# Row factors of the MLP sent by way of HBM, and a new order of work on the last rows

## The reference, cut to what matters

```
def rmsnorm(x, g):
    y = x * rsqrt(mean(x * x, axis=-1) + 1e-6)
    return y * g

x = x + mixed @ w_out                    # mixed: attention and SSM branches, gated
h = rmsnorm(x, g_mlp)                    # x is (512, 1024)
x = x + square(relu(h @ w1)) @ w2        # w1 (1024, 4096), w2 (4096, 1024)
out = rmsnorm(x, g_final)
```

## Time and profile before

| | |
|---|---|
| median of 3 runs | 762.37 us (762.04 to 762.8) |
| the profiled execution | 762.46 us, span 760.6 us |
| granted TensorE clock | 0.999 of full speed |
| PE busy | 744.7 us, 98% of the span |
| DVE busy | 498.1 us, 65% |
| ACT busy | 359.5 us, 47% |
| POOL busy | 54.0 us, 7% |
| HBM | 125 GB/s over the span |

### The profile page before, as it was taken

The page is one execution under the profiler, slowest core; times in us unless marked ns, Lnnn a source line. Parts: engine busy times, 40 slices in busy tenths (PEclk is TensorE's granted clock), DMA queues, the critical chain, the costliest instruction groups (busy, mean ns, idle before and its releaser), DMA issues.

```text
span 760.6 us, 10038 instructions
## 1 busy us (share of the span) xinstructions
PE 744.7 (98%) x3754; PEld 609.2 (80%) x3754; DVE 498.1 (65%) x937; ACT 359.5 (47%) x630; POOL 54.0 (7%) x51
## 2 busy tenths in 40 slices
PE   5999999999999999999999999999999999999996
PEld 4878888777777777888888888888888888888884
DVE  4679999665556673436752667656676567646687
ACT  7524631265556663732421755434443345334454
POOL 3210000000000100000000110011000200020014
PEclk9999999999999999999999999999999999999999
DMA  7673339932223430236238563688177935796322
GB/s 249 197 163 119 100 109 165 202 104 72 70 69 119 159 111 2 84 110 249 84 111 236 124 167 83 166 244 198 56 166 234 229 91 110 196 247 145 83 50 111
DMA packets 99505, 106.19 MB, mean 140 GB/s; under 512 B 10540, under 2 KB 68576, under 8 KB 98432
## 3 DMA queue, kind: packets, MB, share of 16 engines
q1 hardware_dynamic: 93120, 87.05, 40.0%
q0 software_dynamic: 5504, 16.78, 12.1%
q10 hardware_dynamic: 832, 1.71, 1.1%
HBM read 89.70 MB, written 5.34 MB: 125 GB/s over the span
## 4 chain that ended last, share of the span: by engine, by line
PE 93%; DVE 3%; ACT 1%; issue 1%; DMA 1%; POOL 0%; SPq 0%; DVEq 0%; ACTq 0%
PE ps L1642 28%; PE ps L1644 28%; PE ps L1643 27%; PE ps L1932 3%; PE ps L1913 2%; PE ps L1922 1%; DMA mixA<-in_x 1%; PE ps L1717 1%; DVE w_lo L1435 1%; PE ps L1846 1%; ACT w_hi L636 1%; PE ps L1829 1%; DVE x L1484 1%; PE ps L1806 0%; PE ps L1850 0%
## 5 line engine op out<-in xcount | busy, mean ns | idle before, releaser
L1642 PE MATMUL ps<-hT_hi,w_hi 128*128 128x512 f32 x384 | 152.5, 397 | 0.3 <-DVE hT_lo L1004 0.3
L1644 PE MATMUL ps<-hT_hi,w_lo 128*128 128x512 f32 x384 | 149.9, 390 | 0.0
L1643 PE MATMUL ps<-hT_lo,w_hi 128*128 128x512 f32 x384 | 149.5, 389 | 0.0
L1642 PE MATMUL ps<-w_hi,hT_hi 128*128 128x512 f32 x288 | 113.9, 395 | 1.1 <-POOL w_lo L561 1.1
L1644 PE MATMUL ps<-w_hi,hT_lo 128*128 128x512 f32 x288 | 112.3, 390 | 0.0
L1643 PE MATMUL ps<-w_lo,hT_hi 128*128 128x512 f32 x288 | 112.1, 389 | 0.0
L1435 DVE TENSOR_TENSOR w_lo<-raw,w_hi 128x1024 fp32r<-128x1024 f32 x78 | 95.6, 1235 | 22.8 <-ACT w_hi L872 21.5
L872 ACT ACTIVATE w_hi<-raw 128x1024 fp32r<-128x1024 f32 x78 | 81.7, 1052 | 56.2 <-PE ps L1644 56.2
L636 ACT ACTIVATE w_hi<-raw 128x1024 fp32r<-128x1024 f32 x62 | 64.7, 1057 | 57.7 <-PE ps L1644 54.5
L1032 DVE TENSOR_TENSOR w_lo<-raw,w_hi 128x1024 fp32r<-128x1024 f32 x58 | 70.1, 1222 | 31.2 <-ACT w_hi L636 30.6
L1642 PE MATMUL ps<-w_hi,fa_hi 128*128 128x512 f32 x224 | 87.1, 389 | 0.0
(11 more groups left out here) (258 smaller groups left out, 988.5 us busy)
## 6 DMA issues: line engine op xcount, KB each, us to landing
raw<-in_w SPq DMA_DIRECT2D x64, 512.0 KB, 4.9
raw<-in_w_in SPq DMA_DIRECT2D x44, 512.0 KB, 4.9
raw<-raw POOLq DMA_DIRECT2D x8, 1024.0 KB, 6.9
raw<-in_w_glu SPq DMA_DIRECT2D x8, 512.0 KB, 3.8
raw<-in_w_out SPq DMA_DIRECT2D x8, 512.0 KB, 3.7
T_w<-in_w SPq DMA_DIRECT2D x8, 512.0 KB, 6.7
T_w<-in_w POOLq DMA_DIRECT2D x8, 512.0 KB, 7.7
raw<-in_w POOLq DMA_DIRECT2D x8, 512.0 KB, 6.6
```

Of the source, the lines that this page charges most:

```text
L1642: nc.tensor.matmul(dst, a_hi, b_hi, start=start, stop=False)
L1643: nc.tensor.matmul(dst, a_hi, b_lo, start=False, stop=False)
L1644: return nc.tensor.matmul(dst, a_lo, b_hi, start=False, stop=stop)
```

## The change

It has two parts. The first replaces the diagonal tiles, the four matmuls with ones and the copy from PSUM by two DMAs on SP's queue: `rstd2` goes to a 512-element tensor in HBM, and comes back to all 128 partitions. The second changes the end: the two sums of `whole` move from POOL to DVE, `plus_p4(3, 0)` moves ahead of `finish_row(0)`, and row 2 is finished as rows 0 and 1 are.

```diff
@@ SP
-            if c:
+            if c == 0:
+                sp.wait_ge(scale_ready, 1)
+                sp.dma_start(bass.AP(rstd_dram.tensor, 0, [[1, P], [P, TOK]]), rstd2[:, :],
+                             allow_slow_non_contiguous=True).then_inc(rstd_stored, 16)
+                sp.wait_ge(rstd_stored, 16)
+                sp.dma_start(rows_rstd[:, :], bass.AP(rstd_dram.tensor, 0, [[0, P], [1, SEQ]])).then_inc(rows_rstd_set, 16)
+            else:
                 sp.wait_ge(w_lo_done, product_unit(c - 1, 3, 1) + 1)
             for i in range(2):
                 sp.dma_start(T1_w[:, i, :]..., down_source(c, i)).then_inc(t1_in, 16)
@@ SP, stores of the rows: every row waits for out_ready and out_ready_hi
-            if t == 2:
-                sp.wait_ge(row2_ready, 1)
-            else:
-                sp.wait_ge(out_ready, min(t, 2) + 1)
+            sp.wait_ge(out_ready, t + 1)
@@ POOL
-        for t in range(2):
-            pool.wait_ge(p7_joined, t + 1)
-            pool.wait_ge(plus_done, PLUS * (LAST_FF - 1) + 9 + t)
-            nc.gpsimd.tensor_tensor(x2[:, 2 + t, 0:512], x2[:, 2 + t, 0:512], whole[:, t, :],
-                                    ALU.add).then_inc(c21_joined, 1)
@@ ACT
-        act.wait_ge(rstd_spread, 1)
-        nc.scalar.activation(rows_rstd[:, :], ps[:, 2, :], ACT.Identity).then_inc(rows_rstd_set, 1)
...
         scale_out(0)
+        last_stats(2)
         scale_out(1)
-        last_stats(2)
+        scale_out(2)
         last_stats(3)
         scale_out(3)
@@ DVE, join_c21(t) is the sum that POOL made; row_rstd is no longer called by finish_row
+        dve.wait_ge(x_rt, TOK + 1)
+        nc.vector.reciprocal(rstd2[:, :], ms[:, 1, 1, :]).then_inc(scale_ready, 1)
+        up_lo(0, 3)
+        dve.wait_ge(rows_rstd_set, 16)
         dve.wait_ge(mixed_done, 32)
         dve.wait_ge(turned, 2 * KT)
-        nc.vector.memset(ones[:, :], 1.0).then_inc(diag_set, 1)
-        dve.wait_ge(x_rt, TOK + 1)
-        nc.vector.reciprocal(rstd2[:, :], ms[:, 1, 1, :]).then_inc(scale_ready, 1)
-        dve.wait_ge(scale_ready, 1)
-        for t in range(TOK):
-            TS(diag[:, t, :], ident[:, :], rstd2[:, t:t + 1], None, ALU.mult).then_inc(diag_set, 1)
-        up_lo(0, 3)
-        dve.wait_ge(rstd_spread, 1)
-        dve.wait_ge(rows_rstd_set, 1)
...
+        for t in range(2):
+            join_c21(t)
+        plus_p4(LAST_FF, 0)
         dve.wait_ge(gfin_in, 16)
         for t in range(2):
+            row_rstd(t)
             finish_row(t)
-        plus_p4(LAST_FF, 0)
-        gain_rows(dve, TT, 2, rows_gained)
+        row_rstd(2)
         plus_p4(LAST_FF, 1)
-        row_rstd(2)
+        finish_row(2)
         gain_rows(dve, TT, 3, last_gained)
-        dve.wait_ge(rows_gained, 1)
-        TS(x2[:, 2, half_cols(2, 1)], xg[:, 2, :], rstd[:, 2, 2:3], None, ALU.mult).then_inc(out_ready_hi, 1)
-        dve.wait_ge(gained, 3)
-        TS(x2[:, 2, half_cols(2, 0)], x2[:, 2, half_cols(2, 0)], rstd[:, 2, 2:3], None, ALU.mult).then_inc(row2_ready, 1)
         row_rstd(3)
@@ PE: spread_rstd and its call are removed, and the wait of product(0, 2) for rows_rstd_set
```

More of the change, by code:

```diff
@@ L191, in build @@
     fr = sb("fr", [P, 2, SEQ], offset=at["mixA"] + 28672)
-    diag = sb("diag", [P, TOK, P], offset=at["mixA"] + 28672)
-    ones = sb("ones", [P, P], offset=at["mixA"] + 28672 + 2048)
     fs = sb("fs", [P, 2, 2, SEQ], offset=at["CL"])
@@ L204, in build @@
     taps_dram = nc.dram_tensor("taps_dram", [SSM_WIDTH, TAPS * SSM_GROUP], F32, kind="Internal").ap()
+    rstd_dram = nc.dram_tensor("rstd_dram", [TOK, P], F32, kind="Internal").ap()
     frow_dram = nc.dram_tensor("frow_dram", [N_HEADS, SKEW, BIAS_W], F32, kind="Internal").ap()
@@ L211, in build @@
     raw2_in = [sem(f"raw2_in{i}") for i in range(RING)]
-    diag_set = sem("diag_set"); rstd_spread = sem("rstd_spread"); rows_rstd_set = sem("rows_rstd_set")
+    rstd_stored = sem("rstd_stored"); rows_rstd_set = sem("rows_rstd_set")
     f_sum = sem("f_sum"); t1_in = sem("t1_in"); t1_sum = sem("t1_sum"); t2_sum = sem("t2_sum"); t3_sum = sem("t3_sum"); t4_sum = sem("t4_sum"); plus_done = sem("plus_done"); whole_set = sem("whole_set"); p1_joined = sem("p1_joined"); p6_joined = sem("p6_joined")
@@ L252, in build @@
     f_sq = sem("f_sq"); f_lo_done = sem("f_lo_done"); out_ready = sem("out_ready"); gained = sem("gained")
-    rows_gained = sem("rows_gained"); last_gained = sem("last_gained"); row2_ready = sem("row2_ready"); out_ready_hi = sem("out_ready_hi")
+    last_gained = sem("last_gained"); out_ready_hi = sem("out_ready_hi")
     block = ctx.enter_context(nc.Block())
@@ L1542, in row_rstd, with join_c21 @@
             dve.wait_ge(x_rstd, TOK + t + 1)
+        def join_c21(t):
+            dve.wait_ge(p7_joined, t + 1)
+            dve.wait_ge(plus_done, PLUS * (LAST_FF - 1) + 9 + t)
+            TT(x2[:, 2 + t, 0:512], x2[:, 2 + t, 0:512], whole[:, t, :], ALU.add).then_inc(c21_joined, 1)
         def finish_row(t):
-            row_rstd(t)
             cols = half_cols(t, 1)
@@ L1995, in _ @@
                 turn(2, range(0, 4), x2, nat_added, 3 * TOK)
[L1997 to L2002, removed]
         def up(c, n):
@@ L2034, in product @@
                         pe.wait_ge(f_relu, 3 + t)
-                    elif j == 2:
-                        pe.wait_ge(rows_rstd_set, 1)
-                    else:
+                    elif j == 4:
                         pe.wait_ge(hT_lo_done, 2 * KT + t + 1)
@@ L2071, in _ @@
                 up(c, n)
-                if c == 0 and n == 1:
-                    spread_rstd()
             for j in range(PRODUCTS):
```

## The result

The changed kernel takes 771.06 us (median of 5 runs, 770.0 to 772.05), the kernel before 762.47: ratio 1.0109, 95% interval [1.0098, 1.012]. It is 8.6 us slower, where 1.2 us less was forecast. The changed kernel's profiled execution is 771.06 us with a span of 769.3 us, 8.7 more than before.

A forecast was written before the change was run, and what follows sets the result against it. PE, 93% of the chain, was taken to bound the kernel. Removing PE's matmuls (-0.90) and the new end (-0.3), with the round trip causing no stall, sum to -1.2 us: 761.2 us, range 760.1 to 763.6.

The forecast's parts named there:

- I take 2.2, nearest to the quiet row: Store of rstd2 to HBM: priced at 2.2 us after a quiet 64 KB load of 2.0; bounds 0 and 8.5.
- The first rival: HBM round trip lands late and bounds up(0, 6): stall of 4.7 us, 765.9 us at 5 + 5; chance 0.15.
- X: Time when rows_rstd is back from HBM and DVE can go on: forecast 435.15 + 2.2 + 0.05 + 2.2 = 439.6.
- X at most 440.5: Latest return of rows_rstd without PE stalling at up(0, 6), given 17.92 us of DVE and ACT work and 0.1 handover.
- My own upper bounds, 8.5 and 5.0: Dearest landings allowed for the store to HBM and the load back, in us; together they put rows_rstd at 448.7.
- PE gets 0.90 back: Removing the four matmuls with ones moves PE forward by 437.67 - 436.77 = 0.90 us, carried to its end.
- The w2 loads on SP's queue cost nothing: Loads of T1_w and w2 behind SP's waits: costed at 0, with 7 us of cover.
- the second rival: The end gains more: without POOL's sum the last w_lo lets DVE finish 1.1 us earlier, 760.2 us; chance 0.13.
- The end: -0.3 forecast: New order at the end: last store issued 0.12 us later but landing 0.4 us sooner, 2.7 instead of 3.1.

The follow-up runs named there:

- e3: Changed kernel with a dense store, 128 pieces of 16 bytes instead of 512 of 4, columns getting other rows' factors: 762.98 us, ratio 1.0004.
- e4: Kernel before with eight test transfers (five stores, three loads) behind its end, each alone and waited for: 787.05 us in one execution.
- e10: Changed kernel without the HBM round trip, DVE filling rows_rstd with a constant (output not valid): 761.22 us, ratio 0.9989 to the kernel before.
- e5: Changed kernel with SP holding the T1_w and w2 loads until rows_rstd has landed: 768.29 us, ratio 1.0083 to the kernel before.
- e9: Changed kernel with dense store, T1_w and w2 loads held, ACT reordering the row, up_lo(0, 4) ahead of DVE's wait: 760.98 us, ratio 0.9982.
- e2: Kernel before with only the row factors sent by way of HBM, the end in the old order: 770.95 us, ratio 1.0106.
- e11: Kernel before with more test transfers behind its end: 4-byte-piece stores at several spacings and loads to all partitions; 4-byte spacing took 7.9 and 8.2 us.
- e6: Changed kernel with the dense store and relu_f reading the row with a stride of 4 elements: 765.19 us, ratio 1.0039 to the kernel before.

## Why the prediction was wrong

**The step that failed** is "I take 2.2, nearest to the quiet row" for the store, and after it 2.2 for the load: 8.3 and 5.7. The quiet load of the earlier trace rows was near in bytes and traffic, but it is no store of 4-byte pieces into neighbouring places. The argument against the rival, that its dear rows "stood behind other traffic, and here the queue is empty", was true of the store and worth nothing: the queue was empty, and the landing was late with no packet moving. e3 and e4 show it: the same bytes land after 1.4 to 2.0 in pieces of 16. Of the load it was not true: the change itself issues the loads of `T1_w` and w2 0.4 us behind it, and it reads a row that has only just landed. With the two measured landings the prediction's own sum gives X = 435.15 + 8.3 + 0.05 + 5.7 = 449.2.

**The model around it held.** X, in the clock of before, is 450.32 - 1.06 = 449.26. By "X at most 440.5" the stall is 8.8, and `up(0, 6)` starts 8.79 late. The same rule gives 1.8 for e3, where it starts 1.84 late. My own upper bounds, 8.5 and 5.0, give X = 448.7, a stall of 8.2 and 761.2 + 8.2 = 769.4 us: the prediction worked this X out and then left it out of the range. The first rival was the right one, but priced at 5 + 5 (765.9), with a chance of 0.15.

**The price of a transfer by rule.** The fit in the Trainium skill, "DMA: Bandwidth & Descriptors", section "Anatomy of one DMA", gave 2.0 and 2.6; measured 8.3 and 5.7, so the measurement decides. The page gives that fit for DMAs issued by GpSimd; these are SP's, which the prediction did not say. The warnings of the same page that I had quoted (one descriptor per element, read-modify-write under 512 B) pointed the right way; I gave them no price of their own. One descriptor per element agrees with the 528 packets. Neither warning alone gives the price: 512 pieces of 4 bytes, 512 bytes apart, land after 2.1.

**Right, point by point.** PE gets 0.90 back: 0.87 in e10. The w2 loads on SP's queue cost nothing: no gap at the products in the change or in e5, which holds them longer. The last `w_lo` still waits for POOL, now for `gain_first(2)`: 3.44 for the last two `w_lo` in both kernels, so the second rival fell, as the prediction had argued. DVE has no idle time between the four `plus`, the two sums and `plus_p4(3, 0)`. The end: -0.3 forecast, -0.35 in the trace, but its two parts are each a little off and make up for one another: the store goes out 0.06 earlier where 0.12 later was forecast, and lands 0.3 sooner where 0.4 was forecast.

**Not foreseen.** I expected one gap, ahead of `up(0, 6)`. With X this late the nearer demands fail as well, so there were three, with a fall of PE's clock between them; and the start of `up(0, 6)` is still set by the last of them, since DVE's chain of 17.9 us is longer than what PE does in between.

## What to carry to other kernels

A store that is waited for is priced by its pieces and by where they land, not by its bytes: look for a row with the same pieces, and where there is none, keep the dearest bound inside the range. Before a round trip replaces work on the bound engine, compute the latest time at which its result is wanted; here that time (440.5, or 441.6 where `up_lo(0, 4)` stands ahead of the wait) and the landings taken from the traces give the difference to the kernel before for e3, e5, e9 and e10 within 0.4 us, and for the change and e2 within about 1; in e2's trace the fall of the clock behind the last gap is more than that. Lay data out so that the store is dense, and let an idle engine put it in order once, rather than a consumer each time.

## What the runs showed of the hardware

- Stores of 512 4-byte pieces to HBM from 128 partitions: 7.8 to 8.3 us with a step of 4 bytes, 2.5 with 16, 1.8 with 64 and 256, 2.1 with 512. As 128 pieces of 16 bytes next to each other they took 1.4 to 2.0. Why 4-byte neighbours cost so much stays open; that the writes to one stretch of HBM follow each other is a guess.
- A row written by such a store took 5.0 us to be read by all partitions right behind the store, 3.0 when read once more, and 3.3 when first read 6.7 us later (e11, e4).
- A `scalar_tensor_tensor` with one operand read in steps of 16 bytes took 1.05 us instead of 0.69; a copy on ACT so read took 1.11 against the 0.60 of the copy in the kernel before (line 914, which reads PSUM); ACT's 128x512 instruction from SBUF to SBUF in that kernel (line 891) takes 0.63.
- PE's granted clock fell from 2.4 to 1.2 GHz for about 3 us behind the gap ahead of `up(0, 4)` in all three kernels with the slow store, where the gap was 3.38 (the change), 3.04 (e2) and 1.90 us (e5), and in e2 again behind the gap of 1.83. It did not fall behind 2.52 us in e6, 1.84 in the change or 1.65 in e3, so the length of the gap alone does not decide; what does is open. In the change it fell 1.3 us after PE had started again: the clock reads 0.50 of full speed from 454.0 to 456.5, single matmuls went from 0.39 to 0.63 us, and their step from 0.23 to 0.43. There it cost no time, because the next up waited for DVE anyway; in e2 the second fall cost 1.6 us. Two windows of the change (length, PE busy, clock, DMA share, GB/s); the second mixes the two levels:

```profile
439.00:448.80 9.80, 9.80 (x44) 1.00 0.21 20
...
452.20:455.50 3.30, 3.21 (x10) 0.69 1.06 394
```
